# Two-layer hybrid decoder step: merge, feed-forwards and projection as one stage, the norm's statistics made in the residual's epilogue

## The chip, the cores and the metric

One NeuronCore of a Trainium2 chip runs the whole program. The metric is device microseconds of one execution. The kernel before took 4049.2 us (median of three, 4043.1 to 4051.12). TensorE multiplies, VectorE (DVE), ScalarE (ACT) and GpSimd (POOL) do the elementwise work, SyncE (SP) issues most transfers. A TensorE product reads SBUF and writes PSUM; DVE and ACT bring it back.

## What is computed

Two trunk layers over 512 prompt tokens and 64 sample tokens, 576 in all. Each layer is a macaron block:

```python
x = x + 0.5 * swiglu(rms_norm(x, ffn1_norm), w_gate, w_up, w_down)
proj = rms_norm(x, mix_norm) @ w_in           # feeds short conv, RWKV-7, differential attention, gates
merged = g_a * (y_a @ w_a) + g_b * (y_b @ w_b) + g_c * (y_c @ w_c)
x = x + merged @ w_out
x = x + 0.5 * swiglu(rms_norm(x, ffn2_norm), w_gate, w_up, w_down)

def rms_norm(x, w):  return x * rsqrt(mean(x * x) + 1e-6) * w
def swiglu(h, g, u, d):  return (silu(h @ g) * (h @ u)) @ d
```

The model width is 1024, the feed-forward width 2816, everything is float32.

## The kernel before

**Layout.** The residual `x` lies transposed in SBUF as 8 chunks of 128 channels by 576 tokens. A float32 product is made of three fast ones: the weight and the input are each split into a high part (rounded) and a low part (the rest), and `products` (lines 286 to 302) multiplies high by high, low by high and high by low. A unit is one 128-column block of a weight, 8 chunks deep: 48 matmuls of 288 tokens. ACT makes a weight's high part (`split_hi`, line 279), DVE its low part (`split_lo`, line 283). The raw weight, the high and the low part have two buffers each, so the split of unit n+2 can start when unit n has been multiplied. Products go to PSUM tiles `D[0]` and `D[1]`, one for each parity.

**Order.** There is no scheduler: each stage is one Block in which each engine's program is written out, and semaphores tie them. `chase` (line 365) writes the loops of ACT and DVE: for each unit it first splits the next pair's weight of the same parity, then runs the unit's epilogue. Loads of raw weights (`load_w`, line 274) stand on SP's queue and wait only for the buffer. Between two stages stands an all-engine barrier (line 262) that clears all semaphores. The two layers are one hardware loop, `with nc.Fori(0, L) as l`, with 8 stages in it: ffn1, project, prompt attention, sample attention, shifted projection, recurrence, merge, ffn2.

**The norm.** ffn1, ffn2 and project each begin with it: ACT and DVE square the 8 chunks (lines 403 and 417), DVE adds them in pairs (line 420), TensorE sums over partitions with a matrix of ones (line 426, 16 plain float32 matmuls), ACT takes the root (line 410), DVE the reciprocal (line 440). Then DVE makes `hf = x * w * rstd` chunk by chunk (line 449), ACT its high part `h_hi` (line 433), DVE its low part `h_lo` (line 445), and the first unit of the stage waits for each chunk. The final norm (line 2055) is alike.

**The feed-forward.** In two halves of 11 column blocks: gate unit into `D[0]`, up unit into `D[1]`; ACT takes SiLU straight from `D[0]` (line 518), DVE multiplies it with `D[1]` (line 545), ACT and DVE split the product (lines 522 and 548). Then 8 down blocks, each of two units (6 and 5 chunks deep), are added to `x` (line 559). In merge, the 8 units of `w_out` are added to `x` by line 1994.

**The copy of x.** project first stores `x` to DRAM (2.3 MB, line 680), since attention uses its room; merge brings it back.

## Time and profile before

| | |
|---|---|
| three runs, median | 4049.2 us (4043.1 to 4051.12) |
| the profiled execution | 4044.38 us, of which the span is 4042.6 us |
| PE, PEld busy | 91%, 85% of the span |
| DVE, ACT, POOL busy | 39%, 29%, 9% |
| mean granted TensorE clock | 0.946 |
| a 512 KB gate or up weight, issue to landing | 3.8 us (median) |
| instruction fetches (queues q8 and q14) | 142 and 73 packets, 2.93 MB |
| instructions counted | 81476 |

The span runs from the first to the last instruction on the core. "Busy" for PE counts pipelined matmuls, so that a stretch with no gap reads 100% of its length. A row of the timeline gives the start in us, the length in us, the engine, the line, the operation, what it writes and reads, how many, and in brackets how long the engine had been idle and whose work ended that. The seven places where a norm stands are at 35, 479, 1570, 2016, 2467, 3558 and 4004 us.

### The profile page before, as it was taken

How to read it: one execution, taken by the hardware profiler on the slowest of the kernel's cores; microseconds unless marked ns; L12 is line 12 of the kernel's file. 1: busy time of each engine (PE TensorE's matmuls, PEld its weight loads, DVE VectorE, ACT ScalarE, POOL GpSimd, SP SyncE). 2: the span in 40 equal slices, each digit the busy share in tenths (PEclk: the TensorE clock that was granted, in tenths of full speed). 3: DMA queues.
4: the chain of work that ended last, by engine and by line, in shares of the span. 5: the costliest groups of instructions: out<-in, count | busy, mean ns of one | idle time of the engine just before them, and what ended most of it. 6: DMA issues, size and time to landing. Idle time of an engine off the chain costs nothing. (4 is left out here: it accounts for less than half of the span.)

```text
span 4042.6 us, 81476 instructions
## 1 busy us (share of the span) xinstructions
PE 3667.5 (91%) x32956; PEld 3439.9 (85%) x32956; DVE 1566.5 (39%) x2280; ACT 1156.3 (29%) x1829; POOL 369.9 (9%) x602
## 2 busy tenths in 40 slices
PE   6999899888899988999989998997888998989997
PEld 5999898756877788999989997986687777989997
DVE  4332423523544454333343334244244444543333
ACT  2222222333332342222232222133323233322222
POOL 0000003300233200000000000033002331000000
PEclk9999999978999999999989999998889899999998
DMA  2232323372211152222222323234621111422322
GB/s 78 74 87 80 94 74 105 100 260 88 63 33 33 30 167 68 83 83 83 63 79 76 88 76 90 83 107 138 229 73 46 33 44 59 153 65 73 88 77 66
DMA packets 524937, 352.84 MB, mean 87 GB/s; under 512 B 33314, under 2 KB 474572, under 8 KB 523954
## 3 DMA queue, kind: packets, MB, share of 16 engines
q1 hardware_dynamic: 503214, 342.64, 27.8%
q10 hardware_dynamic: 21508, 7.28, 0.7%
q8 instruction: 142, 2.33, 0.2%
q14 instruction: 73, 0.60, 0.0%
HBM read 321.34 MB, written 28.51 MB: 87 GB/s over the span
## 5 line engine op out<-in xcount | busy, mean ns | idle before, releaser
L299 PE MATMUL dense<-h_hi,whi 128*128 128x288 f32 x4032 | 1205.0, 299 | 64.9 <-DVE h_lo L445 58.0
L300 PE MATMUL dense<-h_lo,whi 128*128 128x288 f32 x4032 | 1196.5, 297 | 0.0
L301 PE MATMUL dense<-h_hi,wlo 128*128 128x288 f32 x4032 | 1191.9, 296 | 0.0
L283 DVE TENSOR_TENSOR wlo<-raw,whi 128x1024 fp32r<-128x1024 f32 (+1 forms) x444 | 518.0, 1167 | 1388.1 <-ACT whi L279 1387.9
L279 ACT ACTIVATE whi<-raw 128x1024 fp32r<-128x1024 f32 (+1 forms) x444 | 450.1, 1015 | 1528.8 <-PE dense L301 1457.1
L299 PEld LDWEIGHTS dense<-h_hi,whi 128*128 128x128 f32 x4032 | 761.6, 189 | 72.7 <-issue 60.4
L301 PEld LDWEIGHTS dense<-h_hi,wlo 128*128 128x128 f32 x4032 | 766.3, 190 | 0.0
L300 PEld LDWEIGHTS dense<-h_lo,whi 128*128 128x128 f32 x4032 | 763.9, 189 | 0.0
L299 PE MATMUL dense<-ffn_a_hi,whi 128*128 128x288 f32 x1408 | 416.8, 296 | 0.0
L300 PE MATMUL dense<-ffn_a_lo,whi 128*128 128x288 f32 x1408 | 415.4, 295 | 0.0
L301 PE MATMUL dense<-ffn_a_hi,wlo 128*128 128x288 f32 x1408 | 413.9, 294 | 0.0
L331 PE MATMUL dense<-h_hi,whi 128*128 128x288 f32 x768 | 262.0, 341 | 10.2 <-DVE wlo L317 10.2
L301 PEld LDWEIGHTS dense<-ffn_a_hi,wlo 128*128 128x128 f32 x1408 | 265.2, 188 | 0.0
L300 PEld LDWEIGHTS dense<-ffn_a_lo,whi 128*128 128x128 f32 x1408 | 264.2, 188 | 0.0
L299 PEld LDWEIGHTS dense<-ffn_a_hi,whi 128*128 128x128 f32 x1408 | 263.7, 187 | 0.0
L332 PE MATMUL dense<-h_lo,whi 128*128 128x288 f32 x768 | 230.3, 300 | 0.0
L333 PE MATMUL dense<-h_hi,wlo 128*128 128x288 f32 x768 | 229.8, 299 | 0.0
L269 POOL MEMSET junk<- 128x1 f32 x104 | 4.3, 99 | 2412.6 <-POOLq L262 2412.6
L331 PEld LDWEIGHTS dense<-h_hi,whi 128*128 128x128 f32 x768 | 147.7, 192 | 32.9 <-issue 18.2
L332 PEld LDWEIGHTS dense<-h_lo,whi 128*128 128x128 f32 x768 | 148.7, 194 | 3.9 <-issue 1.4
L333 PEld LDWEIGHTS dense<-h_hi,wlo 128*128 128x128 f32 x768 | 148.3, 193 | 0.0
L299 PE MATMUL dense<-y_hi,whi 128*128 128x288 f32 x384 | 118.7, 309 | 31.5 <-DVE y_lo L1985 21.8
(343 smaller groups left out, 4796.9 us busy)
## 6 DMA issues: line engine op xcount, KB each, us to landing
raw<-in_w_in_dram SPq DMA_DIRECT2D x124, 512.0 KB, 3.9
raw<-in_ffn_w_gate_dram SPq DMA_DIRECT2D x88, 512.0 KB, 3.8
raw<-in_ffn_w_up_dram SPq DMA_DIRECT2D x88, 512.0 KB, 3.8
page<-in_cache_v_dram SPq DMA_DIRECT2D x128, 256.0 KB, 5.5
raw<-in_ffn_w_down_dram SPq DMA_DIRECT2D x64, 384.0 KB, 3.3
page<-in_cache_k_dram SPq DMA_DIRECT2D x96, 256.0 KB, 4.0
raw<-in_ffn_w_down_dram SPq DMA_DIRECT2D x64, 320.0 KB, 3.2
merge_gate<-gates_scratch SPq DMA_DIRECT2D x16, 864.0 KB, 5.2
```

The lines of the kernel that those rows point to most:

```text
L269: pool.memset(self.junk[:, i:i + 1], 0.0).then_inc(s, n)
L279: act.activation(self.whi[s][:, 0:n, :], self.raw[s][:, 0:n, :], ACT.Copy).then_inc(self.w_hi, 1)
L283: dve.tensor_tensor(self.wlo[s][:, 0:n, :], self.raw[s][:, 0:n, :], self.whi[s][:, 0:n, :].bitcast(F32), ALU.subtract)\
L299: pe.matmul(o, w_hi, hi[:, c, t], start=(first and c == 0), stop=False)
L300: pe.matmul(o, w_hi, lo[:, c, t], start=False, stop=False)
L301: mm = pe.matmul(o, w_lo, hi[:, c, t], start=False, stop=(last and c == chunks - 1))
L331: pe.matmul(o, w_hi, self.h_hi[:, c, t], start=(c == 0), stop=False)
L332: pe.matmul(o, w_hi, self.h_lo[:, c, t], start=False, stop=False)
L333: mm = pe.matmul(o, w_lo, self.h_hi[:, c, t], start=False, stop=(c == KD - 1))
```

## The change

1. **Stages joined.** The outer hardware loop over the layers is written out. What were ffn1 + project, then merge + ffn2 + (next layer's) ffn1 + project, then merge + ffn2, are three Blocks `dense0`, `dense1`, `dense2`. Five barriers go (17 become 12). `chase` runs through all segments of a Block, so the next stage's first weights are split during the last units of the stage before.
2. **Squares in the residual's epilogue.** After a chunk of `x` has got its last addition, `tail_act` makes `h_hi = high(x * w)` and the square, `tail_dve` makes `h_lo` and adds the square to an accumulator. Only two float32 matmuls with ones are left for each norm (`stat_pe`).
3. **1/rms on the products.** Before a feed-forward the split input is `x * w` without 1/rms. The gate unit's PSUM is multiplied by `rstd` on DVE, SiLU reads SBUF, SiLU's result is multiplied by `rstd` on DVE and then by the up unit's PSUM: four DVE operations for a pair besides the weight splits, where there were two. TensorE takes `stat_pe` after the first unit of the feed-forward. project still makes `h` from `x * w * rstd`, after `stat_pe`.
4. **The store of x** stands behind the sixth pair of w_in loads instead of ahead of the first.

```diff
-        with nc.Fori(0, L) as l:
-            self.barrier()
-            self.ffn(l, "ffn1")
-            self.barrier()
-            tile = self.region("proj", self.r0 + 36 * KB)
-            self.norm_tiles(tile)
-            self.project(l, "proj", [(0, 12), (COL_Q, 12)], proj)
+        def first_dense(at, steps):
+            return [FeedForward(self, 0, "ffn1", at, steps, None), project(0, at, steps, 1)]
+        def middle_dense(at, steps):
+            return [merge(0, at, steps), FeedForward(self, 0, "ffn2", at, steps, norm_of("ffn1", 1)),
+                    FeedForward(self, 1, "ffn1", at, steps, None), project(1, at, steps, 2)]
+        def last_dense(at, steps):
+            return [merge(1, at, steps), FeedForward(self, 1, "ffn2", at, steps, None)]
+        self.dense("dense0", first_dense)
+        for l in range(L):
+            self.vec = self.vec_all[:, l, 0:NVEC]
+            self.nlam, self.one_li = self.neg_lam[:, l:l + 1], self.lam_init[:, l + L:l + L + 1]
...
-            self.merge(l, y, y_hi, y_lo, m_hi, m_lo, self.region("merge", self.r0 + 40 * KB))
-            self.barrier()
-            self.ffn(l, "ffn2")
+            self.dense(f"dense{l + 1}", (middle_dense, last_dense)[l])
...
-    def norm_dve(self, dve, A, V):
-        for j in range(KD // 2):
-            V.own(dve)
-            V.did(dve.tensor_tensor(self.hf[j % 2][:], self.x[:, 2 * j + 1, :], self.x[:, 2 * j + 1, :], ALU.mult))
-            A.wait(dve, f"sq{j}")
-            V.own(dve)
-            V.did(dve.tensor_tensor(self.sq[j % 2][:], self.sq[j % 2][:], self.hf[j % 2][:], ALU.add), f"pair{j}")
...
+    def tail_act(self, act, c, norm, low, vec):
+        one = lambda t: t[:, ds(c, 1), :].rearrange("p a t -> p (a t)")
+        if vec is not None:
+            act.activation(one(self.h_hi), one(self.x), ACT.Copy, scale=vec[:, ds(c, 1)]).then_inc(self.n_hi, 1)
+        act.wait_ge(self.n_acc, c + ((KD + 1) * norm + 1))
+        act.activation(self.sq[:], one(self.x), ACT.Square).then_inc(self.n_sq, 1)
+    def tail_dve(self, dve, c, norm, low, vec):
+        one = lambda t: t[:, ds(c, 1), :].rearrange("p a t -> p (a t)")
+        if vec is not None:
+            dve.wait_ge(self.n_hi, c + (low + 1))
+            dve.scalar_tensor_tensor(one(self.h_lo), one(self.x), vec[:, ds(c, 1)], one(self.h_hi).bitcast(F32),
+                                     ALU.mult, ALU.subtract).then_inc(self.n_lo, 1)
+        dve.wait_ge(self.n_sq, c + (KD * norm + 1))
+        dve.wait_ge(self.n_acc, c + ((KD + 1) * norm + 1))
+        dve.tensor_tensor(self.acc[:], self.acc[:], self.sq[:], ALU.add).then_inc(self.n_acc, 1)
+    def stat_pe(self, pe, norm, Q):
+        pe.wait_ge(self.n_acc, (KD + 1) * (norm + 1))
+        for half in range(2):
+            mm = pe.matmul(self.E[0][:, half, 0:NH], self.ones[:], self.acc[:, half * NH:(half + 1) * NH],
+                           start=True, stop=True)
+        Q.did(mm, f"stat{norm}")
+    def stat_act(self, act, norm, A, Q):
+        act.preload_act_table_set("sqrt_and_others")
+        Q.wait(act, f"stat{norm}")
+        A.did(act.activation(self.rstd[:].rearrange("p (a t) -> p a t", a=2), self.E[0][:, :, 0:NH], ACT.Sqrt,
+                             bias=self.eps[:, 0:1], scale=1.0 / D), f"root{norm}")
+    def stat_dve(self, dve, norm, A, V, Q):
+        A.wait(dve, f"root{norm}")
+        V.did(dve.reciprocal(self.rstd[:], self.rstd[:]), f"rstd{norm}")
+        Q.wait(dve, f"stat{norm}")
+        dve.memset(self.acc[:], 0.0).then_inc(self.n_acc, 1)
+        V.own(dve)
...
+    def tensor(self, pe):
+        core = self.core
+        def up(f, h, s, ready=None):
+            core.products(pe, f + self.pair[h], s, core.h_hi, core.h_lo, core.D[s], (s, f + (self.used[h] + 1)), ready=ready)
+        for h in range(2):
+            if h == 0:
+                up(0, 0, 0, ready=lambda c: pe.wait_ge(core.n_lo, self.low + c + 1))
+                core.stat_pe(pe, self.norm, self.Q)
+                up(0, 0, 1)
+            with pe.Fori(0, HF - (h == 0)) as f:
+                for s in range(2):
+                    up(f + (h == 0), h, s)
...
+        def begin():
+            core.stat_act(act, self.norm, self.A, self.Q)
+            act.preload_act_table_set("silu_and_others")
+        def silu_and_high(h, f0):
+            def finish(f, j, _, s):
+                act.wait_ge(ev[s], f + (self.used[h] + f0 + 2))
+                if s == 0:
+                    act.activation(self.gate[:], self.gate[:], ACT.Silu).then_inc(core.g_on, 1)
+                    return
+                act.activation(self.a_hi[:, ds(f + f0, 1), :].rearrange("p a t -> p (a t)"), self.prod[:], ACT.Copy)\
+                   .then_inc(core.part_hi, 1)
+            return finish
+        def next_norm(c, u, i, s):
+            if s == 0:
+                return
+            act.wait_ge(ev[u], i + (self.used[1] + HF + 2))
+            core.tail_act(act, c, self.norm + 1, self.low + KD, self.next_vec)
+        none = lambda i, j, c, s: None
+        return [(1, 1, silu_and_high(0, 0), begin), (HF - 1, 1, silu_and_high(0, 1), None), (KD, 2, none, None),
+                (HF, 1, silu_and_high(1, 0), None), (KD, 2, next_norm, None, True)]
...
-                            act.activation(gate[:].rearrange("p (a t) -> p a t", a=2), self.D[0][:, :, 0:NH], ACT.Silu)\
-                               .then_inc(ev[0], 1)
...
-                        dve.wait_ge(ev[0], f + (used[h] + 2))
-                        dve.wait_ge(self.part_lo, f + (h * HF + 1))
-                        dve.tensor_tensor(prod[:].rearrange("p (a t) -> p a t", a=2), self.D[1][:, :, 0:NH],
-                                          gate[:].rearrange("p (a t) -> p a t", a=2), ALU.mult).then_inc(ev[1], 1)
+        def times_up(h, f0):
+            def finish(f, j, _, s):
+                n = f + (h * HF + f0)
+                dve.wait_ge(core.mm_done, f * 2 + (2 * (self.pair[h] + f0) + 3 + s))
+                if s == 0:
+                    dve.tensor_tensor(two(self.gate), core.D[0][:, :, 0:NH], two(core.rstd), ALU.mult).then_inc(ev[0], 1)
+                    return
+                dve.wait_ge(core.g_on, n + (self.gated + 1))
+                dve.wait_ge(core.part_lo, n + (self.part + 1))
+                dve.tensor_tensor(self.prod[:], self.gate[:], core.rstd[:], ALU.mult).then_inc(core.g_two, 1)
+                dve.wait_ge(core.g_two, n + (self.gated + 1))
+                dve.tensor_tensor(two(self.prod), core.D[1][:, :, 0:NH], two(self.prod), ALU.mult).then_inc(ev[1], 1)
+                dve.wait_ge(core.part_hi, n + (self.part + 1))
+                dve.tensor_tensor(self.a_lo[:, ds(f + f0, 1), :].rearrange("p a t -> p (a t)"), self.prod[:],
+                                  self.a_hi[:, ds(f + f0, 1), :].rearrange("p a t -> p (a t)").bitcast(F32),
+                                  ALU.subtract).then_inc(core.part_lo, 1)
+            return finish
+        def add_down(h):
+            def finish(c, u, _, s):
+                if s == 0:
+                    return
+                dve.wait_ge(core.mm_done, c * 2 + (2 * (self.pair[h] + HF) + 4))
+                xs = core.x[:, ds(c, 1), :].rearrange("p a (b t) -> p (a b) t", b=2)
+                dve.scalar_tensor_tensor(xs, core.D[u][:, :, 0:NH], 0.5, xs, ALU.mult, ALU.add).then_inc(ev[u], 1)
+                if h == 1:
+                    core.tail_dve(dve, c, self.norm + 1, self.low + KD, self.next_vec)
...
+            k0 += count // 2
+            if n == 0:
+                sp.dma_start(core.x_d, core.x[:]).then_inc(core.spilled, 16)
+        sp.wait_ge(core.spilled, 16 * self.spills)
...
+        def begin():
+            core.stat_act(act, self.norm, A, self.Q)
+            for c in range(KD):
+                V.wait(act, f"h{c}")
...
+            core.split_hi(act, (n + 2) // 2, n % 2, self.deep(n + 2))
+            if n >= self.branches:
+                act.wait_ge(core.evac[n % 2], n // 2 + 2)
+                core.tail_act(act, n - self.branches, self.norm, self.low, self.next_vec)
...
+            core.split_lo(dve, k + 1, s, self.deep(n + 2))
+            if n >= self.branches:
+                core.tail_dve(dve, n - self.branches, self.norm, self.low, self.next_vec)
...
+            if enter is not None:
+                enter()
+            if written:
+                for i in range(turns):
+                    turn(i)
...
+            def _(act):
+                begins.scalar_first(act)
+                self.chase(act, lambda k, s: self.split_hi(act, k + begins.ahead, s),
+                           [seg for st in stages for seg in st.scalar(act)])
+            def _(dve):
+                dve.memset(self.acc[:], 0.0).then_inc(self.n_acc, 1)
+                begins.vector_first(dve)
+                self.chase(dve, lambda k, s: self.split_lo(dve, k + begins.ahead, s),
+                           [seg for st in stages for seg in st.vector(dve)])
...
-                self.norm_pe(pe, V, Q)
+                for half in range(2):
+                    mm = pe.matmul(self.E[0][:, half, 0:NH], self.ones[:], self.acc[:, half * NH:(half + 1) * NH],
+                                   start=True, stop=True)
+                Q.did(mm, "stat0")
```

How it moves the instructions. First DVE, from the last additions of `w_out` to the next feed-forward's weights, before (`wlo` is a weight's low part, `ffn_sq` the squares, `ffn_hf` the scaled input):

```order
L283 TENSOR_TENSOR wlo_69<-raw_65,whi_67 128x1024 [waits w_hi]
L1994 TENSOR_TENSOR x<-dense,x 128x576 [waits mm_done] x2
L1919 UNCONDITIONAL_BRANCH
L530 UNCONDITIONAL_BRANCH [waits barrier_Pool_Activation_PE_DVE_SP_release]
L417 TENSOR_TENSOR ffn_hf_14539<-x 128x576
L420 TENSOR_TENSOR ffn_sq_14536<-ffn_sq_14536,ffn_hf_14539 128x576 [waits dve_steps,act_steps]
```

and now (`norm_acc` is the accumulator):

```order
L496 TENSOR_TENSOR x<-dense,x 128x576 [waits mm_done]
L644 TENSOR_TENSOR wlo_66<-raw_62,whi_64 128x1024 [waits w_hi]
L767 SCALAR_TENSOR_TENSOR h_lo<-x,vec_all,h_hi 128x576 [waits n_hi]
L771 TENSOR_TENSOR norm_acc<-norm_acc,norm_sq 128x576 [waits n_acc,n_sq]
L789 RECIPROCAL norm_rstd<-norm_rstd 128x576 [waits act_steps]
L791 MEMSET norm_acc 128x576 [waits pe_steps]
L748 UNCONDITIONAL_BRANCH [waits dve_steps]
L644 TENSOR_TENSOR wlo_65<-raw_61,whi_63 128x1024 [waits w_hi]
L292 TENSOR_TENSOR ffn_gate<-dense,norm_rstd 128x576 [waits mm_done]
```

The barrier and the squares are gone from between the additions and the weights; a low part and an accumulation follow each addition.

Second, TensorE at the same place. Before, the norm's sums came after the barrier and ahead of any product; now (last row of `w_out`, first row of the gate unit, which runs for 48 matmuls):

```order
L660 MATMUL dense<-m_hi,whi_64 128x288
L661 MATMUL dense<-m_lo,whi_64 128x288
L662 MATMUL dense<-m_hi,wlo_66 128x288
L660 MATMUL dense<-h_hi,whi_63 128x288 [waits n_lo,evac0,w_split]
L661 MATMUL dense<-h_lo,whi_63 128x288
```

and behind that unit the sums, ahead of the up unit:

```order
L776 MATMUL extra<-norm_acc,ones 128x288 [waits n_acc]
L776 MATMUL extra<-norm_acc,ones 128x288
L660 MATMUL dense<-h_hi,whi_64 128x288 [waits evac1,w_split]
L661 MATMUL dense<-h_lo,whi_64 128x288
L662 MATMUL dense<-h_hi,wlo_66 128x288
```

The first unit no longer waits for the statistics, only for `h_lo` of each chunk.

Third, DVE in the loop over gate and up pairs, before:

```order
L283 TENSOR_TENSOR wlo_68<-raw_64,whi_66 128x1024 [waits w_hi]
L282 REGISTER_ALU
L283 TENSOR_TENSOR wlo_69<-raw_65,whi_67 128x1024 [waits w_hi]
L542 ISA
L543 REGISTER_ALU [waits mm_done]
L545 TENSOR_TENSOR ffn_prod<-dense,ffn_gate 128x576 [waits part_lo,evac0]
L548 ISA [waits part_hi]
L548 TENSOR_TENSOR ffn_a_lo<-ffn_prod,ffn_a_hi 128x576
```

and now:

```order
L644 TENSOR_TENSOR wlo_65<-raw_61,whi_63 128x1024 [waits w_hi]
L290 ISA
L292 TENSOR_TENSOR ffn_gate<-dense,norm_rstd 128x576 [waits mm_done]
L643 REGISTER_ALU
L644 TENSOR_TENSOR wlo_66<-raw_62,whi_64 128x1024 [waits w_hi]
L290 REGISTER_ALU
L294 REGISTER_ALU [waits mm_done]
L295 REGISTER_ALU [waits g_on]
L296 TENSOR_TENSOR ffn_prod<-ffn_gate,norm_rstd 128x576 [waits part_lo]
L298 TENSOR_TENSOR ffn_prod<-dense,ffn_prod 128x576 [waits g_two]
L300 ISA [waits part_hi]
L300 TENSOR_TENSOR ffn_a_lo<-ffn_prod,ffn_a_hi 128x576
```

One operation has come between the two weight splits and one ahead of the product with `D[1]`.

## Rows read from the trace of the kernel before

**Rows 1.** Busy time by stretch: us, PE, PEld, DVE, ACT, POOL (count), PE clock, DMA, GB/s.

```profile
62.00:479.00 417.00, 417.00 (x3130) 416.99 (x3128) 132.40 (x134) 106.31 (x119) 0.00 (x0) 1.00 0.27 78
512.40:1439.40 927.00, 813.26 (x9072) 714.14 (x9071) 366.99 (x683) 285.79 (x578) 183.96 (x282) 0.92 0.29 90
2499.90:3426.90 927.00, 813.76 (x9078) 716.91 (x9078) 367.92 (x683) 285.54 (x577) 184.12 (x282) 0.92 0.29 90
```

**Rows 2.** Waits of TensorE: who for whom, total us, times, longest.

```profile
PE dense L299 <- DVE h_lo L445: 58.0, 22, 10.8
```

**Rows 3.** Timeline, residual product to next feed-forward: start, length, instruction, [idle, releaser].

```profile
1570.42 0.76 DVE L1994 TENSOR_TENSOR x<-dense,x 128x576 f32<-128x576 f32 x1 [5.64 <-PE dense L301]
...
1600.38 1.06 ACT L279 ACTIVATE whi<-raw 128x1024 fp32r<-128x1024 f32 x1 [0.65 <-PE dense L301]
```

**Rows 4.** Timeline, end of the first layer to the second.

```profile
2016.38 0.76 DVE L559 SCALAR_TENSOR_TENSOR x<-dense,x 128x576 f32<-128x576 f32 x1 [5.75 <-PE dense L301]
...
2022.60 1.28 ACT L399 ACT_TABLE_LOAD   x1 [13.90 <-PEq L262]
...
2050.93 1.06 ACT L279 ACTIVATE whi<-raw 128x1024 fp32r<-128x1024 f32 x1 [0.64 <-PE dense L301]
```

**Rows 5.** Timeline, feed-forward to input projection, first layer.

```profile
479.46 0.76 DVE L559 SCALAR_TENSOR_TENSOR x<-dense,x 128x576 f32<-128x576 f32 x1 [5.75 <-PE dense L301]
...
489.71 1.24 PE L426 MATMUL extra<-proj_sq,ones 128*128 128x288 f32 x4 [0.21 <-DVE proj_sq L420]
...
495.15 3.74 DVE L440 RECIPROCAL proj_rstd<-proj_rstd 128x576 f32<-128x576 f32 x1
499.00 1.67 DVE L449 SCALAR_TENSOR_TENSOR proj_hf<-x,vec,proj_rstd 128x576 f32<-128x576 f32 x2
...
512.46 1.06 ACT L279 ACTIVATE whi<-raw 128x1024 fp32r<-128x1024 f32 x1 [1.94 <-PE dense L301]
```

**Rows 6.** Timeline of ScalarE, first feed-forward.

```profile
35.56 1.28 ACT L399 ACT_TABLE_LOAD   x1 [12.97 <-PEq L262]
...
63.47 1.06 ACT L279 ACTIVATE whi<-raw 128x1024 fp32r<-128x1024 f32 x1 [0.64 <-PE dense L301]
```

**Rows 7.** Timeline and chain that ended last, final norm (the x4 row is the chain's).

```profile
4003.78 0.76 DVE L559 SCALAR_TENSOR_TENSOR x<-dense,x 128x576 f32<-128x576 f32 x1 [5.75 <-PE dense L301]
...
4005.68 1.28 ACT L399
...
4008.51 2.30 PE extra L426 x4
...
4015.29 0.74 ACT L410 ACTIVATE final_rstd<-extra,eps 128x576 f32<-128x576 f32 x1 [2.48 <-PE extra L426]
```

**Rows 8.** Groups by line and form: names, shapes, count, busy us, mean ns, idle, releaser.

```profile
L283 DVE TENSOR_TENSOR wlo<-raw,whi 128x1024 fp32r<-128x1024 f32 x396 | 485.0, 1226 | 1343.8 <-ACT whi L279 1343.7
L279 ACT ACTIVATE whi<-raw 128x1024 fp32r<-128x1024 f32 x396 | 419.9, 1061 | 1453.2 <-PE dense L301 1444.7 <-DMA raw<-in_w_in_dram 8.5
...
L545 DVE TENSOR_TENSOR ffn_prod<-dense,ffn_gate 128x576 f32<-128x576 f32 x88 | 66.0, 750 | 0.0
...
L449 DVE SCALAR_TENSOR_TENSOR ffn_hf<-x,vec,ffn_rstd 128x576 f32<-128x576 f32 x32 | 26.2, 819 | 1.4
...
L403 ACT ACTIVATE ffn_sq<-x 128x576 f32<-128x576 f32 x16 | 10.5, 679 | 15.0 <-PE extra L426 14.9
```

**Rows 9.** Timeline inside the second layer's gate and up loop.

```profile
2070.13 1.06 ACT L279 ACTIVATE whi<-raw 128x1024 fp32r<-128x1024 f32 x1 [4.80 <-PE dense L301]
2073.24 0.69 ACT L522 ACTIVATE ffn_a_hi<-ffn_prod 128x576 f32 x1 [2.05 <-DVE ffn_prod L545]
...
2074.09 0.76 DVE L548 TENSOR_TENSOR ffn_a_lo<-ffn_prod,ffn_a_hi 128x576 f32 x1 [0.97 <-ACT ffn_a_hi L522]
```

**Rows 10.** Instruction fetches (packets, MB, share): 62 to 470, then 2017 to 2023 us.

```profile
q8 instruction: 3, 0.05, 0.1%
...
q14 instruction: 8, 0.07, 3.7%
```

570 lines of the change are left out of this document (273 added, 297 removed).

## The prediction

> **What bounds the kernel now.** I first read the busy table by stretch, to see which engine sets the pace. In the long run of a feed-forward TensorE is busy for 417.00 of 417.00 us at a clock of 1.00, while DVE has 132 and ACT 106 us of work [rows 1]. So inside a dense stage only TensorE counts. 3130 matmuls in 417 us are 0.133 us each, so a unit of 48 takes 6.39 us, and all work on DVE and ACT that is done within its unit is free. The stretch between a projection's first unit and merge's first product is 927.0 us in both layers with the same work in it [rows 1]; the change leaves it alone, so I put it at no change.
>
> Next I looked for what TensorE waits for in the dense stages: 58.0 us for the low part of the normed input, 10.8 us the longest [rows 2]. That is only part of the cost of a norm. The timeline shows the whole of it. I measure a seam from the last addition to x (the last product is done just then) to the next stage's first split that waited for TensorE (its first unit is done just then). After a residual product this is 1570.42 to 1600.38, 29.96 us [rows 3], and the same place in the second layer reads alike; from layer to layer 34.55 us [rows 4]; feed-forward to projection 33.00 us [rows 5], alike in the second layer. With one unit's 6.39 us taken off, 23.6, 28.2 and 26.6 us are lost each time. The program's start takes 27.91 us from the barrier to the first unit's end [rows 6], and the final norm 11.51 us from the last addition to the root [rows 7].
>
> **Merge to ffn2, twice.** The barrier, the squares, the root, the reciprocal and the scaled input leave the path. TensorE goes from the last unit of w_out, at T, straight into the gate unit. Weights: this unit's were split after the unit before the last, in time. Input: chunks 1 to 7 are ready. For chunk 8, DVE adds (0.76 us [rows 3]) and splits a weight (1.23 [rows 8]), ACT meanwhile makes the weight's and the chunk's high part (1.06 and about 0.68, the latter by the square's row [rows 8]), and DVE's low part (0.82 by its sister at L449 [rows 8]) ends at about T+3.2. TensorE asks for it after 7/8 of a unit, at T+5.6. No wait. The sums then cost TensorE 1.24 us, by the warm x4 row [rows 5]. The up unit runs to 6.4 us after the sums. In that time ACT takes the root (0.74 [rows 7]), loads SiLU's table (1.28, as the one in [rows 6]) and splits a weight (1.06); DVE takes the reciprocal (3.74 [rows 5]), clears the accumulator, splits (1.23) and multiplies D[0] by rstd (0.75, as L545 [rows 8]). The clearing has no row: 0.1 us from below (hardly any work), 0.75 from above (an addition over the same elements); I take 0.35, since it reads nothing. In a row these give 0.74+3.74+0.35+1.23+0.75, about 6.9 with the hand-overs. TensorE needs D[0] after 6.4, so it waits 0.5 us (0.2 to 0.9). New seam: 6.39+1.24+0.5 = 8.1 us. Gain 21.8 each, **43.7 us**.
>
> **ffn2 to the next ffn1, once.** The same 8.1 us stand against 34.55: **26.4 us**. Here DVE splits the weight ahead of the last addition, so chunk 8's low part comes at about T+4.7, still ahead of T+5.6, and the accumulation ends at T+5.4, ahead of the sums at T+6.4. The seam of before holds an extra: its first ACT instruction starts 6.22 us after the last addition [rows 4], where the final norm's starts after 1.90 [rows 7]. These 4.3 us are the outer loop's jump back; 8 packets came on one fetch queue just then [rows 10]. They go with the loop.
>
> The Trainium skill ("Runtime: NRT & Kernel Launch", Instruction fetch mechanics) says that a taken branch to code outside the two pages at hand stalls for a fetch. By that rule a small loop laid over a page boundary could pay the stall on every turn, which speaks against code that is twice as long; the trace shows no such loop, with 3 packets on the busier queue in 408 us of looping [rows 10]. What it would do is the second rival.
>
> **ffn1 to project, twice.** Only the squares leave this path; h still needs rstd. From T: ACT's weight split 1.06, DVE's 1.23, the addition 0.76, the last square 0.68, the accumulation 0.76: about T+4.65. TensorE has idled for 4.7 us; after an idle of that length the sums took 2.30 us, not 1.24 [rows 7], which is the slower of the clock's two levels, so T+6.95. Root 0.74, reciprocal 3.74, clearing 0.35: T+11.85. From the reciprocal's end to the first unit's end it was 498.89 to 512.46, 13.57 us [rows 5], all set by DVE's two operations for each chunk, and this stays. New seam 25.4 us (24.1 to 26.0). Gain 7.6 each, **15.2 us**. The store of x now leaves behind the sixth pair; a load behind it has about 10 us from its buffer's release to its use, the store about 8 us of transfer, so I put it at nothing; uncovered, it would be 2 us twice.
>
> **The start.** No statistics are needed ahead of the first unit, but DVE and ACT have all 8 chunks to do: low part and accumulation, 0.82+0.76 = 1.6 us a chunk. Two chunks come by 4.0 us after the barrier, then the weights: issued after 0.4 us and landing 3.8 us later, split by ACT and DVE until about 8.2, then six chunks until 17.1; the first unit ends at 17.9, sums and wait 1.75: 19.65 against 27.91. Gain **8.2 us** (4 if the loads land 4 us later, 10 if the two engines overlap better).
>
> **The end.** Addition 0.76, square 0.68, accumulation 0.76, barrier 1.15, sums 2.30 after an idle TensorE: 5.8 against 11.51 [rows 7]. Gain **5.7 us**.
>
> **Inside the stages.** Each of the 88 gate and up pairs gets two DVE operations of 0.75 us more. The one between the weight splits delays SiLU, needed only one unit later. The other lies between the up unit's end and D[1]'s release: ACT's split starts at 2070.13, the high part of the product ends 3.80 us later [rows 9]; 0.8 us more is 4.6, and ACT's next split is due at 6.39. D[1] is free at 3.8, asked for at 6.4. DVE's low part ends at 4.72 now [rows 9], 5.5 then, its next split at 7.5. All is covered, with 1.8 us to spare on ACT. In the last 8 down blocks DVE has two small splits, an addition, a low part and an accumulation, about 3.9 us in 8.8, ACT about 2.9; the next split's turn comes at T+4.8 and ACT is done at T+3.9. Covered, with under a microsecond to spare. So I put both at nothing.
>
> **Sum.** 43.7+26.4+15.2+8.2+5.7 = 99.2 us. Against the profiled execution, 4044.4 - 99.2 = 3945.2 us. The median of the three runs is 4.8 us above the profiled one, their lowest 1.3 below; I take 3 us of that and forecast **3948 us**.
>
> **Rivals.**
> - *The epilogue stretches the units.* In the last down blocks and in w_out, ACT waits for DVE's addition and holds the next weight split behind it. For: the margin of 0.9 us. Against: each length in it is a row. If every block is late by 1 to 2 us, 8 blocks at three seams give back 24 to 48: 3972 to 3996 us. Chance 8%.
> - *Code fetch in loops.* One loop of ACT over a boundary: 4.3 us a turn less 1.8 to spare, 10 turns, 25 us; one to three such loops give 3973 to 4023 us. For: double the code. Against: fetches are rare in loops now [rows 10]. 6%.
> - *Slower than before: the longer chain becomes the loop's bound.* Place: the 88 pairs, from the up unit's end over two splits, two products and the high part. It decides from 1.8 us over what I reckon, and undoes the whole gain from 1.8+99.2/88 = 2.9 us over, when the two new operations take 4.4 us instead of 1.5. At 3.5 us over it gives 3948+1.7*88, 4098 us. For: nothing but that PSUM is read twice as often on DVE. Against: DVE's 0.75 us on a PSUM operand [rows 8], in a loop where it is busy a third of the time. 3%.
> - *Less than it says: the seams stay cold.* If TensorE's waits at the five inner seams let the clock drop, a unit runs at 0.24 instead of 0.133 us a matmul for some microseconds: 3 to 5 us a seam, 3963 to 3973 us. For: after 4.7 us of idling it was slow [rows 7]. Against: the waits that I expect are 0.5 us. 5%.
> - *More than it says*, 3925 to 3935 us, if the start and the joined queues save further. 4%.
>
> **How the numbers follow.** The forecast has 74%. The bounds of its terms (the start 4 to 10, the seams to project 7 to 9 each, the waits 0.2 to 0.9, the median 0 to 5 above the profile) make 3938 to 3962. With the nearest parts of the rivals, 8 in 10 is 3934 to 3974. A measurement of this kernel tells 0.2%, some 8 us, from no change. Faster by more than that: 96%; within it: 1%; slower: 3%.
>
> **What would show it.** In the profile after: no idle of TensorE before the gate unit at the three inner seams, and a first wait of under 1 us ahead of the third unit; the x4 rows of the sums at 1.24 us there and 2.3 ahead of project; project's first unit ending about 25 us after the last addition; ACT's idle before the weight split in the loop at 1.8 instead of 2.6 us. I am wrong if TensorE shows gaps ahead of weights in w_out or the last down blocks, if instruction packets multiply, or if the 927 us stretch moves by more than 2 us.

## The result, and the profile after

The changed kernel takes 3933.7 us (median of 4 runs, 3931.1 to 3937.8) where the kernel before took 4047.4 beside it (median of 4, 4043.1 to 4051.1). The ratio is 0.972, 95% interval 0.971 to 0.973: 113.7 us less, where 99.2 were forecast. The profiled execution of after has 3931.1 us, a span of 3929.3. The time lies 4.3 us below the 3938 that the bounds of the terms allowed and 0.3 us below the 3934 of the wider range; a later measurement of the same kernel gave 3936.1 us (3929.6 to 3938.2), so on which side of 3934 it falls is chance. That it is 14 us below the forecast of 3948 is not.

The first thing to read again is the busy table by stretch, as in [rows 1]; its columns are the same. First a stretch of the first feed-forward, then in each layer the stretch from the projection's first unit to merge's first product.

```profile
54.00:470.00 416.00, 415.43 (x3116) 415.19 (x3115) 174.12 (x187) 116.37 (x128) 0.00 (x0) 1.00 0.28 81
495.40:1416.50 921.10, 811.37 (x9074) 713.58 (x9074) 366.98 (x684) 285.68 (x578) 183.80 (x282) 0.92 0.30 93
2420.10:3342.90 922.80, 813.04 (x9078) 714.96 (x9077) 368.01 (x684) 285.40 (x578) 183.49 (x282) 0.92 0.29 93
```

Inside the feed-forward TensorE is still busy all the time but for one wait of 0.57 us; DVE went from 132 to 174 us of work and TensorE did not wait for it. The other two rows hold the surprise: the stretch that I had put at "no change" is 921.1 and 922.8 us long, not 927.0 twice, with the same products in it. A move of more than 2 us there was one of the signs of being wrong that the prediction names.

TensorE's wait for the low part of the normed input, 58.0 us in [rows 2], is left almost only ahead of the projection. The row of the table of waits:

```profile
PE dense L660 <- DVE h_lo L378: 17.0, 7, 7.5
```

The seam from merge to ffn2, as [rows 3], from three timelines (DVE, PE, ACT), sorted by start:

```profile
1546.33 0.76 DVE L496 TENSOR_TENSOR x<-dense,x 128x576 f32<-128x576 f32 x1 [2.62 <-PE dense L662]
...
1552.53 1.13 PE L776 MATMUL extra<-norm_acc,ones 128*128 128x288 f32 x4
...
1553.70 0.74 ACT L784 ACTIVATE norm_rstd<-extra,eps 128x576 f32<-128x576 f32 x1 [3.70 <-PE extra L776]
...
1554.47 3.75 DVE L789 RECIPROCAL norm_rstd<-norm_rstd 128x576 f32<-128x576 f32 x1 [4.37 <-ACT norm_rstd L784]
1558.30 0.54 DVE L791 MEMSET norm_acc<- 128x576 f32 x1
...
1560.63 0.40 PE L660 MATMUL dense<-h_hi,whi 128*128 128x288 f32 x1 [0.58 <-DVE ffn_gate L292]
```

The last addition starts at 1546.33, which is T, the gate unit runs without a gap, the sums follow it at T+6.2, and the third unit waits 0.58 us for the first PSUM tile, `D[0]` (a "bank" from here on). That is the sequence of the prediction, place by place. The same wait of 0.58 us stands at 1984.82 in the seam from layer to layer.

The seam from ffn1 to the projection, as [rows 5]:

```profile
470.71 1.06 ACT L640 ACTIVATE whi<-raw 128x1024 fp32r<-128x1024 f32 x1 [2.94 <-PE dense L662]
...
475.26 1.74 PE L776 MATMUL extra<-norm_acc,ones 128*128 128x288 f32 x4 [4.64 <-DVE norm_acc L771]
477.04 0.74 ACT L784 ACTIVATE norm_rstd<-extra,eps 128x576 f32<-128x576 f32 x1 [1.33 <-PE extra L776]
477.81 3.75 DVE L789 RECIPROCAL norm_rstd<-norm_rstd 128x576 f32<-128x576 f32 x1 [2.61 <-ACT norm_rstd L784]
...
484.45 0.58 PE L660 MATMUL dense<-h_hi,whi 128*128 128x288 f32 x1 [7.45 <-DVE h_lo L378]
...
495.43 1.06 ACT L640 ACTIVATE whi<-raw 128x1024 fp32r<-128x1024 f32 x1 [1.94 <-PE dense L662]
```

24.7 us from T (470.70) to the end of the first unit (33.0 before); TensorE idles 4.6 us before the sums and 7.5 after them, and its first product then takes 0.58 us instead of 0.30, the next ones 0.44 instead of 0.29. The sums took 1.74 us here and 2.29 us at the same place in the second layer, after the same 4.64 us of idling; 2.30 were forecast for both. The end of the kernel, as [rows 7]:

```profile
3897.41 0.76 DVE L311 SCALAR_TENSOR_TENSOR x<-dense,x 128x576 f32<-128x576 f32 x1 [4.24 <-PE dense L662]
...
3900.62 2.26 PE L2127 MATMUL extra<-norm_acc,ones 128*128 128x288 f32 x4 [3.25 <-PEq L623]
3902.92 0.74 ACT L784 ACTIVATE norm_rstd<-extra,eps 128x576 f32<-128x576 f32 x1 [1.05 <-PE extra L2127]
```

And ACT inside the gate and up loop, as [rows 9]: the high part starts at 1603.24 and the next weight split 1.79 us after its end.

```profile
1603.24 0.69 ACT L267 ACTIVATE ffn_a_hi<-ffn_prod 128x576 f32 x1 [2.86 <-DVE ffn_prod L298]
...
1605.72 1.06 ACT L640 ACTIVATE whi<-raw 128x1024 fp32r<-128x1024 f32 x1 [1.79 <-PE dense L662]
```

Piece by piece, before minus after, from the two profiled executions (T is the last product of a stage):

| piece | forecast | measured |
|---|---|---|
| merge's T to ffn2's T, twice | 43.7 | 21.7 + 21.8 |
| ffn2's T to the next ffn1's T | 26.4 | 26.4 |
| ffn1's T to the projection's first unit, twice | 15.2 | 8.3 + 7.7 |
| barrier to ffn1's T, first layer | 8.2 | 8.3 |
| last T to the final root | 5.7 | 6.0 |
| **these seven** | **99.2** | **100.1** |
| both attentions, recurrence (2 layers) | 0 | 9.2 |
| merge, barrier to T (2 layers) | 0 | 2.7 |
| the rest (before the first barrier, output) | 0 | 1.3 |

The seams are right to 1 us in all. The other 13 us are what has to be explained.

### The profile page after: what moved, and what is told of

Read it like the earlier page. It is cut to its first block and busy times, and to the rows that moved or that the text cites. A ratio compares the mean times of both kernels' runs of the same rounds, so it can differ in the third digit from the quotient of the medians.

```text
span 3929.3 us, 80618 instructions
## 1 busy us (share of the span) xinstructions
PE 3617.9 (92%) x32872; PEld 3406.8 (87%) x32872; DVE 1668.7 (42%) x2427; ACT 1187.2 (30%) x1857; POOL 368.0 (9%) x577
```

## Experiments

Every ratio is to the kernel before, run on the same chip beside the experiment. Two theories of the 13 us: **A**, the change also writes out the loop over the layers, so the layer's number is a constant, and that makes the stages between quicker; **B**, these stages, in which TensorE often stands idle between products ("sparse" below), differ from one execution to the next by themselves, through TensorE's granted clock.

### The loop alone, and repeats of both kernels

```diff
-        with nc.Fori(0, L) as l:
+        for l in range(L):
```

Four runs, in this order: before_unrolled has this edit, rep_before and rep_before2 profile the kernel before again, rep_after the changed one.

> The kernel before with one edit: the loop over the two layers is written out, so the layer's number is a constant in every address; all barriers, norms and stages stay. Theory A (constants in place of a register, and code without the jump back, make attention, recurrence and merge quicker): the jump back goes (4.3 us) and the stages between the projection's first unit and the merge's first product of both layers get some 9 to 12 us shorter, so 13 to 16 us less than before, about 4032. Theory B (those 13 us are the clock's run-to-run play in stages with sparse products, or came from somewhere else in the change): only the jump goes, 4 to 5 us less, about 4043, and the stages keep their lengths within what two executions of one kernel differ by.

> The kernel before, unchanged: a second profiled execution. Theory A: each stage repeats its length within 0.5 us (sample attention 151.6 and 151.5 us, recurrence 361.0 and 361.1 us, merge up to its last product 144.5 and 145.2 us). Theory B: some stage between the projection and the merge differs from the first profile by 2 to 3 us, by a different granted clock there.

> The changed kernel, unchanged: a second profiled execution and its time beside the others of this call. Theory A: the stages repeat within 0.5 us (sample attention 148.5 and 151.7, recurrence 358.3 and 359.5, merge 143.3 and 143.7), the ratio stays 0.972. Theory B: which of the stages is short changes from one execution to the next (in the first one the sample attention of layer 1 was 3.1 us shorter than before and that of layer 2 was not).

> A third profiled execution of the kernel before. If the lengths of the stages play by the granted clock and not by the code: the feed-forwards (445.6, 450.5, 446.0 us) and the projections (180.2) repeat within 0.2 us, sample attention takes 151.6 at a granted clock of 0.78 or 148.5 to 149 at 0.81, the recurrences are anywhere from 356 to 365 us with 40 to 41.5 us of PE idle in each.

Measured: the kernel before with only this edit takes 4032.6 us against 4048.6, ratio 0.996 (0.995 to 0.997), 16 us less (11 to 20). The changed kernel again: 3936.1 us, ratio 0.972 (0.971 to 0.974). The jump between the layers cost about what was forecast: from the barrier ahead of ffn2 to the barrier ahead of the next ffn1 it is 445.7 us without the loop and 450.5 with it, 4.8 less. The row of the second barrier in rep_before2 and in before_unrolled (in brackets the time since the first, less the 0.21 us of the row itself):

```profile
2021.42 0.21 POOL L269 MEMSET junk<- 128x1 f32 x5 [450.25 <-POOLq L262]
```

```profile
2019.55 0.21 POOL L269 MEMSET junk<- 128x1 f32 x5 [445.49 <-POOLq L262]
```

So some 11 us of the 16 (6 to 15) come from elsewhere in the written-out code: theory A's size. But the stages do not repeat either. The table by stretch, sample attention and then recurrence, of the kernel before (first profile, first layer):

```profile
810.63:962.27 151.64, 121.04 (x1192) 84.73 (x1192) 42.24 (x73) 55.66 (x109) 3.85 (x28) 0.78 0.58 200
...
1064.94:1425.96 361.02, 319.88 (x5246) 270.92 (x5246) 156.12 (x313) 116.89 (x267) 113.50 (x159) 0.94 0.14 39
```

its second profile (second layer):

```profile
2800.25:2949.12 148.87, 118.11 (x1192) 83.03 (x1192) 42.23 (x73) 55.66 (x109) 3.84 (x29) 0.81 0.59 204
...
3051.63:3414.67 363.04, 322.60 (x5246) 272.86 (x5246) 156.05 (x313) 116.84 (x267) 113.51 (x159) 0.93 0.14 39
```

and the one with the loop written out (second layer):

```profile
2793.86:2938.90 145.04, 113.89 (x1192) 81.01 (x1192) 42.24 (x73) 55.62 (x109) 3.82 (x29) 0.84 0.61 209
...
3043.11:3401.94 358.83, 322.50 (x5246) 272.71 (x5246) 156.42 (x313) 116.70 (x267) 113.59 (x159) 0.93 0.14 39
```

The same 1192 matmuls take 151.6 us at a granted clock of 0.78, 148.9 at 0.81, 145.0 at 0.84, and one kernel shows more than one of these: the unchanged kernel before had 0.78, 0.78, 0.78, 0.81, 0.81, 0.81 in its three profiles. That is B, and it is why the sample attention of layer 1 looked 3.1 us quicker after the change (0.78 to 0.81) and that of layer 2 did not. The feed-forwards and the projection, at a clock of 1.00 nearly throughout, repeated within 0.5 us.

What doesn't play is the second column against the first: length minus PE busy. In the recurrence it is 41.1 us above, 40.4 in the second profile, 36.3 in the third. Over all profiles of this study:

| recurrence | profiles | executions x layers | length, mean (range) | PE without a product, mean (range) |
|---|---|---|---|---|
| layer in a register | before, 3 profiles | 6 | 362.0 (361.0 to 363.0) | 40.5 (39.9 to 41.1) |
| layer a constant | 11 profiles | 22 | 360.1 (353.5 to 365.0) | 37.9 (36.3 to 39.6) |

The idle times don't overlap: 2.6 us per layer are a property of the code. The lengths do: an execution's length of this stage says nothing about 3 us. The four stages between the projection and merge together took 764.2 us on average with the register (762.2 to 766.7) and 761.0 (754.8 to 766.8; 10 profiles) with the constant, 6.4 us for two layers. Their time without a product does not overlap either: 105.1 us (104.8 to 105.8) against 102.2 (101.2 to 104.0), 5.8 us for two layers, nearly all of it in the recurrence. Both theories hold: of the 9.2 us of the first pair of profiles some 6 are the code; the other 3 are no more than what the lengths play by from one execution to the next.

### Where the constant helps

The recurrence alone in a loop of one turn, around its barrier and its code (rec_register):

```diff
-            self.barrier()
-            self.recurrence(l, z, y, last, ...)
+            with nc.Fori(l, l + 1) as lr:
+                self.barrier()
+                self.recurrence(lr, z, y, last, ...)
```

> The changed kernel with the recurrence alone put in a loop of one turn, so that its DMA addresses are computed from a register again, as in the kernel before; two jumps are added. Over the 24 recurrences profiled so far, PE is without a product for 40.3 to 41.1 us where the layer is a register (4 of them) and for 36.3 to 39.6 us where it is a constant (20). Theory A (register arithmetic ahead of the DMAs on ACT's and SyncE's queues makes that difference): 40 to 41.5 us of idle again in both layers, and with the jumps 6 to 14 us more in all, about 3945. Rival (the shorter idle comes with the written-out code in some other way): idle stays at 36 to 40 us, and only the jumps cost, 0 to 8 us more.

Measured: ratio 0.971 (0.969 to 0.973), 3932.8 us, and PE idle 37.8 us in both layers, as without the loop. That decides nothing, because the edit did not bring the address instructions back: the profile counts 30 instructions more than the changed kernel's, where the edit below took 182 away (a loop of one turn is presumably folded to its constant; no run shows that). The test had to be turned round, the loop kept and the register taken out of the recurrence (rec_const; its second layer computes with the first layer's weights and states, so its outputs are not those of the kernel):

```diff
-            self.recurrence(l, z, y, last, ...)
+            self.recurrence(0, z, y, last, ...)
```

> The kernel before, its loop over the layers kept, with the layer's number in the recurrence alone set to the constant 0: both turns load the first layer's weights and states and store to the first layer's places (the second layer's outputs of this stage are left out, the work is the same). On ACT's queue 26 address instructions go from the program, on SyncE's 12, and nothing else. Theory A (these instructions ahead of the DMAs are what makes PE idle 40.3 to 41.4 us in each of the six recurrences profiled with a register, and 36.3 to 39.6 us in the 22 with constants): the idle falls to 37 to 39 us in both layers; the time falls by 4 to 7 us, about 4041 to 4044. Rival (the shorter idle comes with the code written out twice, its place or its fetching): idle stays at 40 to 41.5 us and the time at that of before.

The recurrence's rows, both layers:

```profile
1062.99:1422.12 359.13, 320.05 (x5246) 270.80 (x5246) 156.52 (x313) 116.90 (x268) 113.53 (x160) 0.94 0.14 39
3045.99:3408.89 362.90, 324.84 (x5246) 275.07 (x5246) 156.51 (x313) 116.84 (x267) 113.57 (x160) 0.93 0.14 39
```

PE is idle for 39.1 and 38.1 us, below all six with the register, and the ratio is 0.9985 (0.9976 to 0.9994), 2 to 10 us less. In the first layer even the addresses are those of the kernel before. So most of the 2.6 us, about 2 by this one profile, is the address arithmetic that ACT and SyncE do before each DMA of a layer's weights and states. (The six with the register span 39.9 to 41.1, a little wider than the expectation says.) The remaining 11 - 6.4 = 5 us of the written-out loop may be nothing. Over the whole execution TensorE is without a product for 366.0 us with the loop written out and for 374.9 to 377.3 us in the three profiles of before: 9.7 us less on average, no more than the jump and the four stages account for. The rest would have to lie in the length of the products themselves, and it is within the interval of the 16 us. Merge can't settle it: barrier to barrier it plays between 145.9 and 149.7 us in the unrolled and looped forms of the kernel before alike.

### What carries the seam

Two edits that each take one half of the seam's design away, and one that splits the stage. By the intervals of the ratios, a difference between two of them is good to some 9 us; the traces are the finer measure. Weights not asked for ahead (ring_wait):

```diff
         core, l = self.core, self.l
+        if self.pair[0] and not self.norm:
+            sp.wait_ge(core.mm_done, 2 * self.pair[0] + 2)
```

> The changed kernel, but SyncE fetches ffn2's first weights only when the merge's last product is done (both layers); norm, squares and the split of x stay in the epilogue. It takes the running-on of the weight queue out of the merge to ffn2 seam and leaves the rest. My theory (the seam's gain needs both, the norm off the path and the queue running on): the first weight lands 3.8 us after its issue, its split takes 1.06 us on ACT and 1.23 us on DVE, so PE idles 6.3 us per seam and then runs some microseconds at the lower clock (in the proj_products run 3.3 us of idle cost 3.1 us more of that kind, in the changed kernel 7.4 us cost 4.6): 2 x 10, so 16 to 22 us more, about 3955. Rival (the epilogue alone carries the gain, the weights would be there anyway): under 4 us more.

```profile
1555.58 0.61 PE L662 MATMUL dense<-h_hi,whi 128*128 128x288 f32 x1 [6.73 <-DVE wlo L646]
```

Ratio 0.976 (0.974 to 0.978), 3953.2 us. TensorE waits 6.7 us for the weight's low part, then works at a clock of 0.50 for the next 3 us and of 0.72 for the 3 after, and reaches the third unit 23.1 us after T, not 14.3: 8.8 per seam, 17.6 for two, by the trace; the two ratios differ by 15 us. The wait is about the reckoned one (6.3), the slow stretch behind it costs 2.1 us and not 3.7. The queue running on is worth 8.8 of the 21.8 us of a seam.

1/rms awaited before the first product (instead of after the first unit, on the products; rstd_waits):

```diff
-            if h == 0:
+            if h == 0 and self.pair[0]:
+                core.stat_pe(pe, self.norm, self.Q)
+                self.V.wait(pe, f"rstd{self.norm}")
                 up(0, 0, 0, ready=...)
-                core.stat_pe(pe, self.norm, self.Q)
                 up(0, 0, 1)
```

(The branch that keeps the old order in the first stage, which has no merge ahead of it, isn't shown.)

> The changed kernel, but at the three seams into a feed-forward inside a dense stage PE makes the sums first and waits for 1/rms before its first product, as if h had to be normalised first; all instructions stay. It prices 1/rms off the path by itself. From the changed kernel's ffn1 to projection seam, where the reciprocal ends 10.9 us after the last product and the cold unit behind it takes 11.0 instead of 6.4 us: 3 x (10.9 + 4.6) = 46 us more, about 3981. Rival (most of the chain ran beside other work even before, and only the 3.75 us of the reciprocal are late): 3 x 4 to 6, 12 to 18 us more.

```profile
1555.72 2.04 PE L781 MATMUL extra<-norm_acc,ones 128*128 128x288 f32 x4 [3.86 <-DVE norm_acc L776]
1562.38 0.61 PE L665 MATMUL dense<-h_hi,whi 128*128 128x288 f32 x1 [4.62 <-DVE norm_rstd L794]
```

Ratio 0.981 (0.979 to 0.983), 3974.2 us: 36 us by the ratios, 3 x 11.9 = 36 by the length of the middle dense stage (1189.6 against 1165.8 us, two seams). I had 46: the first product comes 10.5 us after T, as reckoned, but the slow unit behind it loses under 2 us, not 4.6. What I had taken over from the projection's cold unit was mostly its waiting for h, chunk by chunk. Both halves are needed: without the queue running on 8.8 of the 21.8 us go, without the deferred 1/rms 11.9. No run takes both away.

The middle dense stage cut between the layers (split_layer):

```diff
-            return [merge(0, at, steps), FeedForward(self, 0, "ffn2", at, steps, norm_of("ffn1", 1)),
-                    FeedForward(self, 1, "ffn1", at, steps, None), project(1, at, steps, 2)]
+            return [merge(0, at, steps), FeedForward(self, 0, "ffn2", at, steps, None)]
+        def second_dense(at, steps):
+            return [FeedForward(self, 1, "ffn1", at, steps, None), project(1, at, steps, 1)]
...
+            if l == 0:
+                self.barrier()
+                self.dense("dense3", second_dense)
```

> The changed kernel with the middle dense stage cut in two between the layers: ffn2 of layer 1 ends with a barrier and ffn1 of layer 2 begins with its own squares and split of x, as the first one does. The layer to layer seam gained 26.4 us, of which the jump back is 4.3 to 4.8 (still gone here) and the quicker begin of ffn1 8.2 (still here): 13.5 us more, about 3949. If the joined stage gave its gain by something else (the queues, the code's length), it is under 8 or over 20 us.

Ratio 0.976 (0.974 to 0.977), 3950.6 us: 14 us by the ratios. From T to the third unit it is 28.9 us against 14.3, 14.6 more. The parts of the layer seam (jump 4.8, quicker begin 8.2, joined stage 14) add up to 27 us, of 26.4 gained.

### How much room the up loop has

The product of gate and 1/rms made m+1 times, m = 2 and 4, on DVE between the up unit's end and the release of the second bank, `D[1]` (up_extra2 and up_extra4):

```diff
-                dve.tensor_tensor(prod, gate, rstd, ALU.mult).then_inc(core.g_two, 1)
-                dve.wait_ge(core.g_two, n + (self.gated + 1))
+                for j in range(m + 1):
+                    dve.tensor_tensor(prod, gate, rstd, ALU.mult).then_inc(core.g_two, 1)
+                    dve.wait_ge(core.g_two, n * (m + 1) + (self.gated * (m + 1) + j + 1))
```

> The changed kernel with the product of gate and 1/rms made three times instead of once (2 x 0.79 us more per pair). The second bank is free at 3.95 + 1.58 = 5.5 us of 6.4: no change, within 3 us. Rival (ACT's next split is the bound from 1.8 us on, or each added DVE operation costs at once): 15 us more or above.

> The changed kernel with the product of gate and 1/rms made five times instead of once in the up loops, on DVE (4 x 0.79 us more per pair, 88 pairs; same result). In the changed kernel DVE frees the second PSUM bank 3.95 us after the unit's end, and PE needs it after 6.4: 2.45 us of room. With 3.16 us more the bank is 0.7 us late in each pair: 88 x 0.7 = 62 us more, about 3998. Rival of the prediction (the 1.8 us before ACT's next weight split are the room, and everything over it is lost): 88 x (3.16 - 1.8) = 120 us more. If the chain had no influence at all: no change.

With two more: ratio 0.973 (0.971 to 0.974), 3939.7 us, the changed kernel's within the interval; no wait of TensorE in the loop, 65.00 us busy in a window of 65. With four more: ratio 0.996 (0.995 to 0.997), 96 us given back. One turn of it, and the sum of these waits:

```profile
1614.38 0.37 PE L661 MATMUL dense<-h_hi,whi 128*128 128x288 f32 x1 [0.74 <-DVE ffn_prod L299]
```

```profile
PE dense L661 <- DVE ffn_prod L299: 59.9, 80, 1.0
```

The wait is the reckoned one, 0.74 us (0.7), at the reckoned place; the bank decides and not ACT's 1.8 us. (Two more products, 1.6 us, lie under both limits and could not have told them apart.) In the other 8 of the 88 turns, the last of each half, TensorE waits up to 0.8 us for the product's low part. But 96 us were given back and not 62, mostly because the loop's turn grew from 12.8 to 13.8 us. Matmuls that follow each other every 0.133 us take 0.29 us each, overlapped; the record's gap begins at the end of the last, 0.16 us after the next could have started, and the first after the gap takes 0.37. A gap of 0.74 us in the trace costs 1.0 us. And these waits do not lower the clock: it stays at 1.00.

### A version that beats both

The projection was the one stage that still waited for h. Its first pairs of units can be treated as the feed-forward's (proj_products with two pairs, proj_three with three): the epilogue of ffn1 splits x times the mix_norm vector into a buffer of its own, the first units multiply that and are scaled by 1/rms when they leave PSUM, and the normalised split that attention needs later is made beside them.

```diff
+        for k in range(2):          # 3 in the second form
+            for s in range(2):
+                core.products(pe, k + self.pair, s, core.u_hi, core.u_lo, core.D[s], ...)
+                if k == s == 0:
+                    core.stat_pe(pe, self.norm, self.Q)
-        with pe.Fori(0, self.pairs) as k:
+        with pe.Fori(0, self.pairs - 2) as k:
...
+            dve.tensor_tensor(two(self.dest[:, 2 * k + s, :]), core.D[s][:, :, 0:NH], two(core.rstd[:]), ALU.mult)
```

> The changed kernel with the projection's start treated as the feed-forward's: the residual's epilogue of ffn1 also makes the split of x times the mix_norm vector (in a buffer of its own), the projection's first two pairs of units multiply that and are scaled by 1/rms as they leave PSUM, and the normalised split that attention and the shifted projection need is made beside them, ready for the third pair. In the changed kernel 24.7 and 25.3 us pass from ffn1's last product to the end of the projection's first unit, 13.8 of them idle on the tensor engine and the rest at 11.0 for a unit that takes 6.4 warm. If the seam's length is the serial chain of sums, root, reciprocal and h (my theory of the seams), the unit now follows without a gap: 24.7 - 6.4 - 1.2 of sums = 17.1 us less per layer, 34 in all, about 3900. Rival: the added scaling and h chain (8 x 2.2 us on DVE and ACT) are late for the third pair, and a part of the gain, 3 to 10 us per layer, comes back there as a wait on h_lo.

Measured 3915.7 us, ratio 0.967 (0.966 to 0.969): 20 us less than the changed kernel, not 34. The rival of the expectation came true in its size, 7 us per layer, but not in its place: the wait is not for the low part of h. First the gap before the third pair, then the stretches behind it:

```profile
502.17 0.61 PE L682 MATMUL dense<-h_hi,whi 128*128 128x288 f32 x1 [3.31 <-DVE proj L406]
```

```profile
501.50:505.00 3.50, 2.83 (x12) 2.83 (x13) 2.42 (x3) 0.00 (x0) 0.00 (x0) 0.50 0.53 157
505.00:508.00 3.00, 3.00 (x14) 3.00 (x14) 0.00 (x0) 0.00 (x0) 0.00 (x0) 0.50 0.61 172
508.00:511.50 3.50, 3.50 (x28) 3.50 (x27) 0.00 (x0) 0.00 (x0) 0.00 (x0) 0.97 0.00 0
```

DVE did all remaining chunks of h before the third pair's weight split, which ended at 501.5, and emptied the first bank only behind that split. During the wait of 3.3 us the clock went down to 0.50, and the next 6 us lost another 3. Three pairs instead of two, with the chunks spread between the weight splits:

> As proj_products, but the first three pairs of the projection multiply the unnormalised split, the normalised chunks are spread over the gaps between the weight splits of these pairs, and the first bank is emptied before norm_acc is cleared. In proj_products the weight split of the third pair stood behind the chain of h chunks: PE idled 3.3 us before it and then 10.0 instead of 6.4 us went into the unit at the lower clock, and 0.5 to 0.8 us before the second pair. With these gone the seam is 17 us shorter than in the changed kernel instead of 10: 34 us less in all, about 3902, 14 less than proj_products. Rival (the third or a later pair is late again, by the same DVE work in another place): 3908 to 3918.

```profile
484.92 0.37 PE L686 MATMUL dense<-u_hi,whi 128*128 128x288 f32 x1 [0.58 <-DVE proj L407]
```

Measured 3901.5 us (3893.5 to 3907.7), ratio 0.963 (0.962 to 0.965). The 0.58 us above is the only wait left at this seam (and at that of the second layer), and the first dense stage is 592.4 us long against 609.2: 16.8 less, 17.1 expected.

## Why the prediction was right, and where it fell short

**What bounds the kernel; the seams.** Right. Each seam is a serial chain of lengths that nearly all stood in rows of the kernel before, and each measured gain is within 0.8 us of the forecast one. The largest miss, 16.0 for 15.2 us ahead of the two projections, has its place: the first layer's sums took 1.74 us and not 2.30. rstd_waits and ring_wait show that both the deferred 1/rms and the queue carry the gain; the two terms that no row had measured, DVE's clearing (0.54 us, taken as 0.35) and the wait it adds (0.58, taken as 0.5), moved nothing. Three of the sums are not quite those of their own terms: the end's lengths add up to 5.65 us and not 5.8, those ahead of project's sums to 4.5 and not 4.65, and at the start six chunks of 1.6 us behind 8.2 end at 17.8 and not 17.1. The last was luck: ACT and DVE made a chunk every 1.5 us, and the start's gain was 8.3 us for 8.2.

**Inside the stages.** Right: no wait in the gate and up loops, 1.79 us of ACT's idle time where 1.8 were forecast. Of the room I named the wrong limit: not ACT's 1.8 us but the bank's 2.4, as up_extra4 shows (3.2 us added, and in 80 of the 88 turns TensorE waits for the bank, at a cost of 1.0 us). up_extra2 shows that 1.6 us more are free.

**Code fetch in loops.** Didn't happen. The page's rows of the two instruction queues after the change (packets, MB, share):

```profile
q8 instruction: 143, 2.34, 0.2%
q14 instruction: 61, 0.50, 0.0%
```

The kernel before, whose slice is in [rows 10], fetched 142 and 73 packets in all, and 140 and 61 with only its loop written out: hardly fewer, so the loop over two layers must have fetched its body twice anyway. In the first feed-forward of the changed kernel 4 and 3 packets came in 416 us of looping, where 3 and 2 came in 408 us before; no small loop fetched on each turn. The Trainium skill ("Runtime: NRT & Kernel Launch", Instruction fetch mechanics) says that a taken branch out of the two pages at hand forces a fetch. The packets agree for the outer loop; that a small loop stalls by this rule no run here shows.

**The step that failed** is "the change leaves it alone, so I put it at no change", of the 927 us stretch. The diff does touch these stages: their DMAs' addresses were computed from the layer's register on ACT's and SyncE's queues, and are constants now. I had priced the loop by its jump alone (4.3 us; 4.8 measured). Written out by itself it is worth 16 us (11 to 20), of which 4.8 are the jump and some 6 were found in the four stages and traced in the recurrence, for the most part, to the address arithmetic; whether the rest is real stays open. With that term the sum would have been 99 + 11 = 110 us, and the forecast 3937. The last 3 us are within the play of the sparse stages, which no row of one profile could tell: the first profile's two layers happened to agree on 927.0. I read that as a property of the stretch; it was two equal draws, as the four stages in it took 762.2 to 766.7 us over three profiles of the same kernel. The range was too tight at its lower end for the same reason: it held no play of the stages at all.

**The rival "more than it says"** had the right time (3925 to 3935) by the wrong cause, the start and the joined queues; these came out as forecast. That it holds the measured time is luck.

## What to carry to other kernels

A factor that is common to a column can be applied after the product, and then the statistics that give it have a whole unit of time; but the full gain needs the weight queue to run on across the seam as well: without it 8.8 of 21.8 us were lost here. When a loop is written out, look in every stage at what was computed from its register, above all ahead of DMAs. A profile of one execution gives a stage of sparse matmuls to about 3 to 5% only (353.5 to 365.0 us, 144.8 to 151.7 us): compare the idle time, which repeats better, and the granted clock beside it.

## What the runs showed of the hardware

- Sparse stages run at lengths that go with the granted clock of the execution, not with the program: 151.6 us at 0.78, 148.9 at 0.81, 145.0 at 0.84 for the same 1192 matmuls.
- A pause of 0.6 to 1.0 us left the clock at 1.00 (up_extra4, proj_products); one of 3.3 us was followed by some 6 us at 0.50, and the time lost after it was as long as the pause. The loss does not grow with the pause: one of 6.7 us cost 2.1 us more behind it (ring_wait).
- A gap of 0.74 us in the record of a stream of pipelined matmuls costs 1.0 us (up_extra4, a turn of 13.8 us for 12.8).
- Writing a two-turn loop out, twice the code, left the instruction fetches where they were (201 packets for 215; 204 in the changed kernel).
- Register address arithmetic ahead of DMAs: 26 instructions on ACT and 12 on SyncE in the program of a stage of 360 us (182 fewer counted over two layers without them) made TensorE idle about 2 us longer (40.5 against 38.6 us, one profile of rec_const).
